# Ring of three places for split weights, halves made two chunks ahead, and the tables' split one chunk later, in a fused two-block forward pass on one Trainium2 core

## The reference

```python
for i in range(2):                       # first block
    u = rms_norm(h, norm_mix_g[i]); proj = u @ w_in[i]         # 1024 -> 6656
    y_a = multiscale_pool(a_in, ...); y_b = c_b * conv(c_c * c_x); y_c = diff_attention(...)
    merged = g_a * (y_a @ w_pool_out[i]) + g_b * (y_b @ w_conv_out[i]) + g_c * (y_c @ w_attn_out[i])
    h = h + merged @ w_o[i]
    h = h + square(relu(rms_norm(h, g) @ w_up[i])) @ w_down[i]  # 1024 -> 4096 -> 1024
    h = h + sigmoid(rms_norm(h, g) @ w_ple_gate[i]) * (p[i] @ w_ple_proj[i])
# second block, depth 2, with adaptive modulation
x = x + g1 * attention_mixer(modulate(x), modulate(ctx), ...)   # MLA and GQA heads
x = x + g2 * sq_relu_mlp(modulate(x), w1[0], w2[0])
x = x + g1 * hyena_mixer(modulate(x), ...)   # z = short_conv(h @ w_in); FFT convolutions, order 2
x = x + g2 * sq_relu_mlp(modulate(x), w1[1], w2[1])
return rmsnorm(x, final_g)
```

## Time and profile before

| | |
|---|---|
| time, median of 3 runs | 3493.21 us (3483.47 to 3497.33) |
| the profiled execution's own time | 3497.29 us |
| its span in the profile | 3495.3 us |
| mean granted TensorE clock | 0.972 of full |
| TensorE busy with matmuls | 3312.2 us, 95% |
| VectorE, ScalarE, GpSimd busy | 59%, 35%, 18% |
| HBM read | 328.00 MB, 97 GB/s over the span |
| chain that ended last, by engine | PE 71%, VectorE 12%, GpSimd 10%, ScalarE 4% |

### The profile page before, as it was taken

One profiled execution on the slowest core, in us unless ns is written; L12 is line 12 of the kernel. 1 busy time (PEld: TensorE's weight loads), 2 busy tenths in 40 slices (PEclk: granted clock), 3 DMA queues, 4 the chain that ended last, 5 costly groups with the idle time before them and its releaser, 6 DMA issues.

```text
span 3495.3 us, 36820 instructions
## 1 busy us (share of the span) xinstructions
PE 3312.2 (95%) x15132; PEld 2659.0 (76%) x15132; DVE 2053.7 (59%) x2663; ACT 1210.5 (35%) x1647; POOL 643.5 (18%) x495
## 2 busy tenths in 40 slices
PE   7999999999999999999988999989999888889998
PEld 5877777888787777888866776767778767777887
DVE  6655657664765565777557456564554567764443
ACT  3234442224433444222432333333343332333222
POOL 0000000000100003999610000003332023210000
PEclk9999999999999999999999899999999989899999
DMA  2222234542222223454311010022333221122222
GB/s 103 88 85 85 69 131 179 195 178 95 86 82 87 77 73 140 181 193 181 114 67 37 17 40 1 34 82 96 115 143 111 109 85 62 71 73 97 97 97 72
DMA packets 55623, 342.95 MB, mean 98 GB/s; under 512 B 5984, under 2 KB 7328, under 8 KB 18208
## 3 DMA queue, kind: packets, MB, share of 16 engines
q1 hardware_dynamic: 54080, 337.98, 26.9%
q10 hardware_dynamic: 1376, 2.62, 0.2%
HBM read 328.00 MB, written 12.58 MB: 97 GB/s over the span
## 4 chain that ended last, share of the span: by engine, by line
PE 71%; DVE 12%; POOL 10%; ACT 4%; issue 2%; DMA 0%; DVEq 0%; ACTq 0%; POOLq 0%
PE PS L262 69%; POOL FA L271 9%; DVE wl L271 2%; DVE FA L279 2%; PE PS L265 1%; DVE UL L271 1%; ACT wh L268 1%; DVE SC L279 1%; ACT SC L268 1%; DVE SC L288 1%; DVE SC L271 1%; ACT UH L268 1%; DVE FA L271 1%; DVE FA L288 1%; ACT FA L268 1%
## 5 line engine op out<-in xcount | busy, mean ns | idle before, releaser
L262 PE MATMUL PS<-UH,wh 128*128 128x512 f32 x2072 | 833.9, 402 | 42.6 <-DVE wl L271 21.6
L271 DVE TENSOR_TENSOR wl<-raw,wh 128x2048 fp32r<-128x2048 f32 (+2 forms) x255 | 560.3, 2197 | 446.1 <-ACT wh L268 446.0
L262 PE MATMUL PS<-UH,wl 128*128 128x512 f32 x2072 | 812.4, 392 | 0.0
L262 PE MATMUL PS<-UL,wh 128*128 128x512 f32 x2072 | 812.4, 392 | 0.0
L262 PE MATMUL PS<-RH,wh 128*128 128x512 f32 (+2 forms) x1688 | 672.4, 398 | 62.5 <-DVE UL L271 28.1
L262 PE MATMUL PS<-RL,wh 128*128 128x512 f32 (+2 forms) x1688 | 661.5, 392 | 0.0
L262 PE MATMUL PS<-RH,wl 128*128 128x512 f32 (+2 forms) x1688 | 661.3, 392 | 0.0
L268 ACT ACTIVATE wh<-raw 128x2048 fp32r<-128x2048 f32 (+2 forms) x255 | 454.6, 1783 | 320.1 <-PE PS L262 317.7
L262 PEld LDWEIGHTS PS<-UH,wh 128*128 128x128 f32 x2072 | 392.6, 189 | 160.0 <-issue 27.0
L262 PEld LDWEIGHTS PS<-UL,wh 128*128 128x128 f32 x2072 | 393.0, 190 | 84.4 <-issue 6.3
L262 PEld LDWEIGHTS PS<-UH,wl 128*128 128x128 f32 x2072 | 392.4, 189 | 83.6
(11 more groups left out here) (191 smaller groups left out, 3308.4 us busy)
## 6 DMA issues: line engine op xcount, KB each, us to landing
raw<-in_wall SPq DMA_DIRECT2D x224, 1024.0 KB, 4.8
FA<-in_wmod SPq DMA_DIRECT2D x48, 1024.0 KB, 4.8
raw<-in_wall SPq DMA_DIRECT2D x29, 512.0 KB, 3.5
kspec<-FA SPq DMA_DIRECT2D x8, 1024.0 KB, 7.5
FA<-kspec SPq DMA_DIRECT2D x8, 1024.0 KB, 4.8
PB<-in_window SPq DMA_DIRECT2D x16, 256.0 KB, 4.4
raw<-in_wall SPq DMA_DIRECT2D x8, 272.0 KB, 2.6
Hs<-in_xT ACTq DMA_DIRECT2D x4, 512.0 KB, 10.4
```

Of the source, the lines that this page charges most:

```text
L262: return self.put(self.eng and self.eng.matmul(out, w, x, start=start, stop=stop, skip_group_check=True))
L271: return self.put(self.eng and self.eng.tensor_tensor(out, a, b, op))
```

## The change

`wh` and `wl` become rings of three places (PLACES = 3), which takes 16 KB more of each partition of SBUF; the program is built with `dynamic_dma_scratch_size=1024`. `raw` stays a ring of two. `w_hi` and `w_lo` make halves up to two chunks ahead of their tag, and wait for the `sum` of the chunk three places before. A new test, `blocked`, ends a call ahead of an unsplit load that lies between the tag and the next half. The second calls at the end of each Hyena chunk are taken out. The load of the tables `cs`, and so their split, moves from behind ("up", 2, 0, 1) to behind ("dn", 2, 0, 0) in the plan. The matmuls, their order and the weights are the same.

```diff
--- before.py
+++ after.py
@@ -17,6 +17,7 @@
 EPS = 1e-6
 RAWN = 2048
 RAWS = 2
+PLACES = 3
 NEG = -1e30
 TWO_PI = 2.0 * math.pi
 
@@ -142,10 +143,10 @@
         for q in range(4):
             for j in range(4):
                 load(("up", M, q, j), ("sum", ("up", M, q, 2 * j + 1)), piece(up, l, 0, 8, 1024 * q + 256 * j, 256))
-                if M == 2 and q == 0 and j == 1:
-                    load(("cs",), ("sum", ("sv", 3, 1, 3)), *[piece(n, None, 0, 4, 0, 256) for n in ("C", "S")], split="own")
             for j in range(4):
                 load(("dn", M, q, j), ("sum", ("dn", M, q, 2 * j + 1)), piece(down, l, 1024 * q, 8, 256 * j, 256))
+                if M == 2 and q == 0 and j == 0:
+                    load(("cs",), ("sum", ("sv", 3, 1, 3)), *[piece(n, None, 0, 4, 0, 256) for n in ("C", "S")], split="own")
 
     for l in range(2):
         for i, c0 in enumerate((2048, 2304, 2560, 2816)):
@@ -328,8 +329,8 @@
     Hs, HB = twice("Hs", "HB", [128, 8, S])
     return dict(
         FA=FA, FB=FB, Hs=Hs, HB=HB, UH=sb("UH", [128, 8, S], FR), UL=sb("UL", [128, 8, S], FR),
-        raw=sb("raw", [128, RAWS * RAWN]), wh=sb("wh", [128, RAWS * RAWN], FR),
-        wl=sb("wl", [128, RAWS * RAWN], FR),
+        raw=sb("raw", [128, RAWS * RAWN]), wh=sb("wh", [128, PLACES * RAWN], FR),
+        wl=sb("wl", [128, PLACES * RAWN], FR),
         RH=sb("RH", [128, 8, S], FR), RL=sb("RL", [128, 8, S], FR),
         SC=sb("SC", [128, 4, 528]), PB=sb("PB", [128, 2304]), PR=sb("PR", [128, NP]),
         CO=sb("CO", [128, sum(CWIDTH)]), ST=sb("ST", [128, 8, 8]), MOD=sb("MOD", [128, 2, 48, 2]),
@@ -422,7 +423,7 @@
         if tag == ("ct",):
             return HB[:, o:o + n], HB[:, 2048 + o:2048 + o + n]
         i = index[tag]
-        a = (place[i] % RAWS) * RAWN + o
+        a = (place[i] % PLACES) * RAWN + o
         return (wh[0:plan[i][2], a:a + n], wl[0:plan[i][2], a:a + n])
 
     SSQ = PB[:, 1792:2304]
@@ -1167,9 +1168,13 @@
         done = [0]
         two = Turns([0, 1])
 
-        def w_hi(tag, ahead=1):
-
-            while done[0] < len(halves_of) and before(halves_of[done[0]]) <= place[index[tag]] + ahead:
+        def blocked(tag):
+
+            return any(plan[x][4] is False for x in range(index[tag] + 1, halves_of[done[0]] - 1))
+
+        def w_hi(tag, ahead=2):
+
+            while done[0] < len(halves_of) and before(halves_of[done[0]]) <= place[index[tag]] + ahead and not blocked(tag):
                 i = halves_of[done[0]]
                 t = plan[i][0]
                 a.wait_ge("raw%d" % (i % RAWS), t)
@@ -1178,8 +1183,8 @@
                 elif t == ("ct",):
                     a.wait_ge("spill", 0)
                     a.wait_ge("u_w", (8, 7))
-                elif place[i] >= RAWS:
-                    a.wait_ge(*plan[ring[place[i] - RAWS]][5])
+                elif place[i] >= PLACES:
+                    a.wait_ge(*plan[ring[place[i] - PLACES]][5])
                 a.activation(pair(t, 0, plan[i][3])[0], whole(t), ACT.Copy).then_inc("w_hi", t)
                 done[0] += 1
 
@@ -1680,8 +1685,6 @@
                         a.activation(sc(s, 8, 520), sc(s, 8, 520), ACT.Identity, bias=ST[:, 5, m:m + 1])
                         a.settle()
                         a.activation(conv_tile(k), sc(s, 8, 520), ACT.Identity, **middle).then_inc("hw", (0, m))
-                if j < 11:
-                    w_hi(("hw", j + 1))
 
             def signal(s):
                 od, hf = STEPS[s]
@@ -1790,9 +1793,12 @@
         done = [0]
         pairs = Turns([2, 3])
 
-        def w_lo(tag, ahead=1):
-
-            while done[0] < len(halves_of) and before(halves_of[done[0]]) <= place[index[tag]] + ahead:
+        def blocked(tag):
+            return any(plan[x][4] is False for x in range(index[tag] + 1, halves_of[done[0]] - 1))
+
+        def w_lo(tag, ahead=2):
+
+            while done[0] < len(halves_of) and before(halves_of[done[0]]) <= place[index[tag]] + ahead and not blocked(tag):
                 i = halves_of[done[0]]
                 t = plan[i][0]
                 h, lo = pair(t, 0, plan[i][3])
@@ -2435,8 +2441,6 @@
                     v.stt(y, sc(x, 7, 519), col("h_conv_w_2", 0, k), y, MUL, ADD)
                     v.settle()
                     v.stt(y, sc(x, 9, 521), col("h_conv_w_2", 0, 48 + k), y, MUL, ADD).then_inc("hw_y", k)
-                if j < 11:
-                    w_lo(("hw", j + 1))
 
             def signal(s):
                 for t4 in range(4):
@@ -2908,7 +2912,7 @@
             c += width
     arrays["wall"] = wall
 
-    nc = _bacc.Bacc("TRN2", target_bir_lowering=False, num_devices=1)
+    nc = _bacc.Bacc("TRN2", target_bir_lowering=False, num_devices=1, dynamic_dma_scratch_size=1024)
     aps = {n: nc.dram_tensor("in_" + n, list(a.shape), _mybir.dt.float32, kind="ExternalInput").ap()
            for n, a in arrays.items()}
     aps["out"] = nc.dram_tensor("outT", [D, S], _mybir.dt.float32, kind="ExternalOutput").ap()
```

## The result

The changed kernel took 3476.92 us in the median of 9 runs (3468.80 to 3483.42), the kernel before 3493.21 (9 runs, 3483.47 to 3501.66). The ratio is 0.995, with a 95% interval of 0.9934 to 0.9967: 16.3 us less, about 0.5%. The forecast was 3476. The profiled execution has a span of 3474.9 us at a mean clock of 0.974, against 3495.3.

What follows compares the result with a forecast made beforehand. TensorE was taken to bound the kernel, busy 3312.2 of 3495.3 us, so only its gaps and clock count. The terms sum to -17.5 us from 3497.3, giving 3479.8, or 3476 on the medians' scale; range 3453 to 3496.

Steps and rivals of the forecast that it cites:

- (b): Merge and output projection, twice: wl's wait goes but wo0's half delays the last merge products; +5.5 us, bounds -4 and +8.
- (c): Start of an MLP's downs, first block: wl waits go, hidden tiles' splits end last; +0.5 us, bounds -2 and +2.
- (d): End of second MLP: copies queued past SP's wait delay the last adds and the norm's sums; +7.5 us, bounds 0 and +11.
- (e): Gates and the second block's attention: TensorE's chunks cover the moved halves; -0.5 us, bounds -2 and +4.5.
- (f): Third MLP's start: the tables leave and gaps for splits and wl shrink; -4 us, bounds -7 and -1.
- (g): Hyena's start: the wl wait goes, the UL wait shrinks, less half clock follows; -10 us, bounds -12 and -5.
- (h): Hyena's body: halves move ahead of convolutions, shortening the chain and raising the inverse's clock; -15.3 us, bounds -22 and -6.
- (i): Last MLP: a wl wait of 2.70 us and one of 0.8 go; -3.5 us, bounds -4 and -1.
- (1): Rival, whole kernel: all 33.1 us of wl waits go, half clock too, without losses before Hyena; 3460 us, chance 0.15.
- (2): Rival, Hyena: the half delays the convolutions as much as it frees behind, clock stays; 3491 us, chance 0.12.
- (3): Rival, Hyena: halves ahead of convolutions delay each of 11 chunks by 2.36 us; 3517 us, chance 0.10.
- (4): Rival, whole kernel: two raw places and unsplit loads hold halves to one ahead; no gain, 3493 us, chance 0.05.

Runs made afterwards that it cites:

- One ahead: Changed kernel with halves made one chunk ahead in the whole first block, two ahead from chunk kv on: 3462.26 us, ratio 0.9917 to the kernel before.
- The experiment on SP's order: Changed kernel with SP's wait for the pooling features, and three transfers, moved behind the second layer's load pg0: 3471.08 us, ratio 0.9938.
- the third experiment: Changed kernel with each Hyena chunk's halves made behind its convolutions again, still in the ring of three: 3497.05 us, ratio 1.0012.
- the last experiment: Kernel one ahead in the first block, with Hyena's halves from chunk 4 made in odd chunks alone: 3442.56 us, ratio 0.9860.

## Why the prediction was right

The sum was -17.5 us against the profiled execution; the medians differ by 16.3, the spans by 20.5. By its own steps, size by size, with the stages' wandering in mind:

- **What the change does to the order** held. wl waits went but for the first, and UL from L272 kept its 61 us, though by other waits: 8.5 us at the three odd inverses and 3.4 at Hyena's start are gone, and 5.3 at the first down chunk, 3.4 in the third MLP and 1.3 more at each of two even inverses are among those that came.
- **(a)**: +2.3 forecast. The gap rose from 1.65 to 3.85 us; the stage's time wanders by more than that.
- **(b)**: +5.5. The first one is +2.6 by the table. TensorE's last gap ends at 459.29 in a trace 2.3 us late, which is the 457.0 of the forecast. The second, cut out of the row from 600 to 1700, is +2.3 from 1300 to 1400, with gaps of 4.78 and 1.14 us: 4.9 in all. One ahead takes all of it back.
- **(c)**: +0.5, measured +1.4 in the first MLP. It was mis-sized: UL came no earlier, as said, but TensorE had stood for 4.25 us, and the 14.4 us from 555.60 on ran at a mean clock of 0.71, where it was 1.00 from 548.00 to 558.90 before. That clock was not in the term.
- **(d)**: +7.5, measured +9.8. The gap of 6.79 us was sized well (+7.4 for the last split, from 1732.0 to 1752.0 in a trace 11.6 us late: +8.4); the clock behind it (0.73 from 1751.5 to 1765, 1.00 from 1731 to 1745 before) is the rest. The experiment on SP's order shows that the queue past SP's wait was the cause.
- **(e)**: -0.5, measured -4.7, outside its bounds of -2 and +4.5 and the term most off. Most of it is one stretch of the attention, where the clock was 0.71 from 1904 to 1925 before and 1.00 from 1926 to 1942 after. All kernels with two ahead there show 2.4 to 6.9 us of it, four with the same code up to there among them, so that the size is open; the tables' move alone shows 0.6. Which gap keeps the clock up was not tried.
- **(f)**: -4, measured -4.6: -7.8 up to 2330 and +3.2 behind. The gap at 2366 did not go, though the signs said that it would; its wait has become one for UL, and a second of 0.58 us follows:

```profile
2369.41 0.55 PE L263 MATMUL PS<-UH,wh 128*128 128x512 f32 x1 [2.82 <-DVE UL L272]
```

- **(g)**: -10, measured -11.3.
- **(h)**: -15.3, measured -15.3. That the two are the same is luck. The odd chunks gave -15.9 instead of -12.8 and the rest +0.6 instead of -2.5, and kernels with the old order in this stage lie between -2.9 and +2.1 themselves.
- **(i)**: -3.5, measured -5.9, outside its bounds of -4 and -1. Round the gap named it is -3.4; another -1.6 lies from 3105 to 3130, and the kernel with the tables moved alone has -3.2 there, with the same code as before.

The gains sum to 42 instead of 33 and the losses to 21 instead of 16, so errors stood on both sides and cancelled in part. The order of events was foreseen; that the number came within 1 us of 3476 is luck. Two slips in the working are too small to matter: three times 1.7 is 5.1 and not 5.3 in (h), and the upper bounds add to +15.0 and not +15.5. The sign of being wrong, that UL's waits grow by what wl's lose, did not come: with L280 they grew by 10.6 us, against 26.4 lost.

Of the rivals, (1) fell: part of the gaps came back under another name. (2) fell with the third experiment: the order on VectorE was worth 12 to 17 us. (3), that the halves delay the convolutions, was right in its mechanism in the even chunks, where the wait for UL grew by 1.3 us and the last experiment found some 13 us, and wrong in the odd ones. (4) fell, since the waits for wl went; but its premise, that raw loads end no copy's wait, holds no longer in the first block, where they end most of it.

The trace has the half of an even chunk at 3.38 us beside GpSimd, against 2.29. The rule on shared interfaces in the Trainium skill (GPSIMD Engine Reference, Specifications), which stood beside (h), agrees with that. By it (h) was to end near its small end of -6, and it did not, since the odd chunks' halves lay where GpSimd had no work (it stood idle for 14.18 us up to 2870.13 in the changed kernel); the contention bore on the even chunks alone. The odd inverse went from a clock of 0.76 to 1.00 with its gaps gone. The rule on waits between bursts in the Trainium skill (TensorE: Matmul & The Clock Gate, "HAM oscillation — how this bites in real kernels") agrees with that.

## What to carry to other kernels

Making something a step earlier on an engine that runs in order also moves it ahead of whatever stood before it: look for each place where that other work is what the next engine waits for, and for each queue in which its inputs stand. A deeper buffer is worth having where the early work falls into an idle stretch of its engine; where it doesn't, keep the shallow distance there, stage by stage. The table of waits names the last releaser and does not price it: taking 26 us of waits for wl away was worth 16 us here, while a kernel that left 21 us of them in place was faster. And a stage that one profile shows some us faster can be so by chance: compare kernels whose code is the same there.

## What the runs showed of the hardware

VectorE's operations with two operands in SBUF take longer beside GpSimd, and GpSimd's beside them: a 128x2048 subtraction 3.38 us instead of 2.29, a 128x512 GpSimd operation 3.35 instead of 1.28. What GpSimd would lose had not been expected. TensorE's clock was lower behind two short waits: those of 1.78 and 1.06 us, with three matmuls between them, were followed by a mean of 0.76 over 7.2 us, where the same inverse without them ran at 1.00. One wait of 1.48 us with dense work on both sides was followed by a mean of 1.00 from 548.00 to 558.90.
